# Per-head transposes of a retention and HGRN kernel moved from TensorE to 32x32 turns by VectorE and a permuting DMA

## The reference, cut to what matters

```
s = s * c_dec + einsum('bhjd,bhjv->bhdv', kc * k_dec, vc)                       # retention state
s = exp(b_last)[..., None] * s + einsum('bhjd,bhjv->bhdv', kc * exp(b_last - b), vc)  # HGRN state
o_r = merge(rms_norm(o_rf + flip(o_rb))) * silu(rg)
o_h = merge(rms_norm(o_hf + flip(o_hb), hg_norm_w)) * silu(hg)
out = concatenate([o_r, o_h], axis=-1) @ w_out
y   = rms_norm(x + gate * out, final_norm_w)
```

## Time and profile before

| What | Value |
|---|---|
| Median of 3 runs (lowest to highest) | 1424.56 us (1424.13 to 1424.7) |
| Span of the profiled execution, first to last instruction | 1422.8 us |
| What the runs have around that span | 1.8 us (1424.56 - 1422.8) |
| TensorE busy | 1406.0 us, 99% |
| VectorE busy | 970.9 us, 68% |
| ScalarE busy | 496.9 us, 35% |
| GpSimd busy | 367.9 us, 26% |
| Mean granted TensorE clock | 0.999 of 2.4 GHz |
| DMA of SP's queue | 195.15 MB in 68736 packets, 39.8% of 16 engines |

### The profile page before, as it was taken

The page is one execution under the profiler, slowest core; times in us unless marked ns, Lnnn a source line. Parts: engine busy times, 40 slices in busy tenths (PEclk is TensorE's granted clock), DMA queues, the critical chain, the costliest instruction groups (busy, mean ns, idle before and its releaser), DMA issues.

```text
span 1422.8 us, 24874 instructions
## 1 busy us (share of the span) xinstructions
PE 1406.0 (99%) x10232; PEld 1186.6 (83%) x10232; DVE 970.9 (68%) x1293; ACT 496.9 (35%) x894; POOL 367.9 (26%) x292
## 2 busy tenths in 40 slices
PE   7999999999999999999999999999999999999997
PEld 5788898889888988898889888988898888888886
DVE  5655666666689778877887788866676668632345
ACT  4333343334333433343334233423342334321234
POOL 0000115311532153215321532153115315301220
PEclk9999999999999999999999999999999999999999
DMA  9994222322333334333432343222223347183235
GB/s 387 417 419 148 89 83 82 90 96 67 127 122 123 97 126 133 113 97 126 134 111 97 127 135 110 97 97 90 82 69 96 89 154 254 46 288 111 89 104 206
DMA packets 68870, 196.66 MB, mean 138 GB/s; under 512 B 7824, under 2 KB 16288, under 8 KB 63904
## 3 DMA queue, kind: packets, MB, share of 16 engines
q1 hardware_dynamic: 68736, 195.15, 39.8%
q10 hardware_dynamic: 32, 0.02, 0.0%
HBM read 174.41 MB, written 16.53 MB: 134 GB/s over the span
## 4 chain that ended last, share of the span: by engine, by line
PE 96%; DMA 3%; DVE 1%; SPq 0%; issue 0%; ACT 0%; DVEq 0%; ACTq 0%
PE ps L2044 10%; PE ps L2046 10%; PE ps L2045 10%; PE ps L1867 9%; PE ps L1869 8%; PE ps L1868 8%; PE ps L1843 8%; PE ps L2227 5%; PE ps L2229 5%; PE ps L2228 5%; DMA area<-in_w_mod 3%; PE ps L2061 2%; PE ps L1876 2%; PE ps L1874 2%; PE ps L1875 2%; PE ps L1833 2%
## 5 line engine op out<-in xcount | busy, mean ns | idle before, releaser
L1151 DVE TENSOR_TENSOR w_lo<-area,w_hi 128x1024 fp32r<-128x1024 f32 x143 | 182.9, 1279 | 254.6 <-ACT w_hi L679 254.5
L679 ACT ACTIVATE w_hi<-area 128x1024 fp32r<-128x1024 f32 x143 | 151.6, 1060 | 501.8 <-PE ps L2046 292.5
L2044 PE MATMUL ps<-w_hi,hT_hi 128*128 128x512 f32 x640 | 252.1, 394 | 0.0
L2046 PE MATMUL ps<-w_hi,hT_lo 128*128 128x512 f32 x640 | 249.3, 390 | 0.0
L2045 PE MATMUL ps<-w_lo,hT_hi 128*128 128x512 f32 x640 | 249.3, 389 | 0.0
L1867 PE MATMUL ps<-hT_hi,w_hi 128*128 128x512 f32 x512 | 205.5, 401 | 0.0
L1868 PE MATMUL ps<-hT_lo,w_hi 128*128 128x512 f32 x512 | 199.8, 390 | 0.0
L1869 PE MATMUL ps<-hT_hi,w_lo 128*128 128x512 f32 x512 | 199.7, 390 | 0.0
L2046 PEld LDWEIGHTS ps<-w_hi,hT_lo 128*128 128x128 f32 x640 | 120.1, 188 | 25.4
L1735 POOL TENSOR_TENSOR area<-area 128x320 f32<-128x320 f32 x56 | 53.0, 947 | 339.5 <-PE ps L2061 287.1
L2044 PEld LDWEIGHTS ps<-w_hi,hT_hi 128*128 128x128 f32 x640 | 120.2, 188 | 24.3
(11 more groups left out here) (287 smaller groups left out, 2466.4 us busy)
## 6 DMA issues: line engine op xcount, KB each, us to landing
area<-in_w_in SPq DMA_DIRECT2D x144, 512.0 KB, 4.0
area<-in_w_mod SPq DMA_DIRECT2D x26, 1024.0 KB, 12.4
area<-in_w_out SPq DMA_DIRECT2D x38, 512.0 KB, 3.7
gate_raw<-in_w_gate SPq DMA_DIRECT2D x32, 512.0 KB, 3.7
gate_raw<-in_w_mod SPq DMA_DIRECT2D x6, 1024.0 KB, 12.1
o_hi_scratch<-area SPq DMA_DIRECT2D x14, 320.0 KB, 2.2
o_lo_scratch<-area SPq DMA_DIRECT2D x14, 320.0 KB, 2.9
hT_hi<-o_hi_scratch SPq DMA_DIRECT2D x14, 320.0 KB, 7.4
```

What stands on the lines that cost most here:

```text
L679: act.activation(split_weights(h, n)[0], raw[:, n % 3, :], ACT.Copy).then_inc(wt_hi.sem, 1)
L1151: v.tensor_tensor(lo, raw[:, n % 3, :], hi.bitcast(F32), ALU.subtract).then_inc(wt_lo.sem, 1)
L2044: mm(out, hT_hi[:, k, tile_cols(t)], w_hi[:, n % 2, w], start=k == 0, stop=False)
L2046: i = mm(out, hT_lo[:, k, tile_cols(t)], w_hi[:, n % 2, w], start=False, stop=k == KT - 1)
```

## The change

For heads 0 to 6 the 18 transposes on TensorE go away. Head 7 keeps them. In their place:

- VectorE turns each 32x32 block of the decayed keys in place of its own block (`turn_keys`: 512, 128 and 384 columns into `rope`), at the end of item 17. SP then (`move_keys`, item 4, behind the load of chunk 4) stores `rope` to DRAM (512 KB in rows of 4 KB), waits for it, and reads it back with 4 DMAs that put the blocks in their places in `kltok`, in runs of 32 numbers (128 B), 1024 runs each.
- VectorE turns the 32x32 blocks of the gated outputs (`retention_turn` at item 3, `hgrn_turn` at item 13; 640 columns each) into `o_one`. ScalarE rounds them into `o_two`, VectorE subtracts in place, and SP stores the two parts with 4 DMAs each, one per quarter of the partitions, in runs of 128 B, 640 runs each.
- TensorE does `chunk_updates` behind the retention outputs after chunk 1, and waits there for the moved keys. Waits for the removed pieces go, and some that they carried move to their neighbours.

```
+        k_dram = nc.dram_tensor("key_scratch", (P, 8 * P), F32).ap()
...
+            def store_turned(row, stored):
+                for dram, buf in ((o_hi_dram, o_two), (o_lo_dram, o_one)):
+                    out = dram[bass.ds(row, 1)].rearrange("h (c i) (t q j) -> q i (h t) c j", c=QUARTERS, q=QUARTERS, j=QUAD)
+                    for q in range(QUARTERS):
+                        sp.dma_start(out[q], buf[q * QUAD:(q + 1) * QUAD, :].rearrange("p (t c j) -> p t c j", c=QUARTERS, j=QUAD)
+                                     ).then_inc(stored.sem, 16)
+            def move_keys(h):
+                sp.wait_ge(k_turned.sem, k_turned.at(h))
+                sp.dma_start(k_dram, rope).then_inc(k_moved.sem, 16)
+                sp.wait_ge(k_moved.sem, k_moved.at(h, 16))
+                sp.wait_ge(r_kt.sem, r_kt.at(h))
+                turned = k_dram.rearrange("(q j) (t c i) -> c j t q i", q=QUARTERS, c=QUARTERS, i=QUAD)
+                for c_ in range(QUARTERS):
+                    sp.dma_start(kltok[c_ * QUAD:(c_ + 1) * QUAD].rearrange("p t (q i) -> p t q i", q=QUARTERS), turned[c_]
+                                 ).then_inc(k_moved.sem, 16)
...
                 if n == 4 and prev is not None:
+                    move_keys(prev)
                     store_states(prev, n_ret_f, n_ret_b, rst, r_state, r_state_stored)
...
                 if n == 8 and prev is not None:
-                    sp.wait_ge(r_low.sem, r_low.at(prev))
-                    sp.dma_start(o_hi_dram[bass.ds(prev, 1)].rearrange("h d t -> (h d) t"), o_one).then_inc(r_stored.sem, 16)
-                    sp.dma_start(o_lo_dram[bass.ds(prev, 1)].rearrange("h d t -> (h d) t"), o_two).then_inc(r_stored.sem, 16)
+                    sp.wait_ge(o_split.sem, o_split.at(prev, 1))
+                    store_turned(prev, r_stored)
...
                 if n == 17 and prev is not None:
-                    sp.wait_ge(h_low.sem, h_low.at(prev))
...
+                    sp.wait_ge(o_split.sem, o_split.at(prev))
+                    store_turned(prev + HEADS, h_stored)
...
+            def turned_high(h, k):
+                act.wait_ge(o_turned.sem, o_turned.at(h, k))
+                act.wait_ge(h_silu.sem, h_silu.at(h, 4))
+                act.activation(o_two_r, o_one, ACT.Copy).then_inc(o_rounded.sem, 1)
...
+            def retention_turn(h):
+                dve.wait_ge(r_gated.sem, r_gated.at(h))
+                v.transpose(o_one, sT).then_inc(o_turned.sem, 1)
+            def hgrn_turn(h):
+                dve.wait_ge(h_gated.sem, h_gated.at(h))
+                dve.wait_ge(r_stored.sem, r_stored.at(h))
+                v.transpose(o_one, hsT).then_inc(o_turned.sem, 1)
+            def turned_low(h, k):
+                dve.wait_ge(o_rounded.sem, o_rounded.at(h, k))
+                v.tensor_tensor(o_one_r, o_one, o_two, ALU.subtract).then_inc(o_split.sem, 1)
+            def turn_keys(h):
+                dve.wait_ge(h_kl.sem, h_kl.at(h))
+                v.transpose(rope[:, 0:4 * P], KL[:, 0, 0:4 * P])
+                v.transpose(rope[:, 4 * P:5 * P], KL[:, 1, 0:P])
+                v.transpose(rope[:, 5 * P:8 * P], KL[:, 1, 2 * P:T]).then_inc(k_turned.sem, 1)
...
                     tokens_last(h)
+                    if not isinstance(h, int) or h < HEADS - 1:
+                        turn_keys(h)
...
             def chunk_updates(h):
-                pe.wait_ge(h_kltok.sem, h_kltok.at(h))
+                if h == HEADS - 1:
+                    pe.wait_ge(last_keys.sem, last_keys.at(0))
+                else:
+                    pe.wait_ge(k_moved.sem, k_moved.at(h))
+                    pe.wait_ge(r_S.sem, r_S.at(h))
+                    pe.wait_ge(r_state.sem, r_state.at(h))
...
                     if n == 1:
                         retention_outputs(prev, A, BB)
-                        key_tokens(prev)
-                    if n == 2:
                         chunk_updates(prev)
                     if n == 3:
-                        retention_columns(prev, h)
                         level_scores(prev, h, 0)
                         level_scores(prev, h, 1)
...
-                    if n == 13:
-                        pe.wait_ge(ctx_copied.sem, ctx_copied.at(h))
-                        hgrn_columns(prev, h)
```

More of the change, by code:

```diff
@@ L317, in layer @@
         h_sq, h_rms, h_gated = Signal("h_sq"), Signal("h_rms", 2), Signal("h_gated")
[L318 to L321, removed]
+        last_keys, pe_hu, pe_level = Signal("last_keys", 2), Signal("pe_hu"), Signal("pe_level", PRODUCTS)
+        pe_ho = Signal("pe_ho")
+        h_S0, h_stored, h_state_stored = Signal("h_S0", 32), Signal("h_stored", 2 * QUARTERS * 16), Signal("h_state_stored", 32)
         o_landed = [Signal(f"o_landed{j}", 32 if j % 4 == 3 else 64) for j in range(WCHUNKS)]
@@ L727, in group_columns @@
                     act.wait_ge(pe_group.sem, pe_group.at(h, s + 1))
-                    if due(pe_hkl, h - 1):
-                        act.wait_ge(pe_hkl.sem, pe_hkl.at(h - 1))
+                    if due(k_turned, h - 1):
+                        act.wait_ge(k_turned.sem, k_turned.at(h - 1))
                     act.activation(KL[:, s, P:T], ps[:, GROUP_BANKS[s], :], ACT.Exp, scale=-1.0).then_inc(h_ez.sem, 1)
@@ L812, in keys @@
             def keys(h):
-                act.wait_ge(pe_hkl.sem, pe_hkl.at(h))
+                act.wait_ge(last_keys.sem, last_keys.at(0, 1))
                 act.activation(kltok[:, 0:4, :], tiles(ps[:, C, :]), ACT.Copy)
-                act.activation(kltok[:, 4:8, :], tiles(ps[:, DD, :]), ACT.Copy).then_inc(h_kltok.sem, 1)
+                act.activation(kltok[:, 4:8, :], tiles(ps[:, DD, :]), ACT.Copy).then_inc(last_keys.sem, 1)
             def context_states(h):
@@ L852, in hgrn_high @@
             def hgrn_high(h, out, context):
-                act.wait_ge(pe_ht.sem, pe_ht.at(h))
+                act.wait_ge(pe_columns.sem, pe_columns.at(0))
                 act.activation(out[:, P:T], ps[:, A, :], ACT.Copy)
@@ L887, in items @@
                     if n == 2:
-                        keys(prev)
                         retention_norm(prev, A, BB)
-                    if n == 3:
                         context_states(prev)
                     if n == 4:
-                        retention_high(prev, o_one_r, ctx_columns(h)).then_inc(r_high.sem, 1)
+                        turned_high(prev, 1)
                     if n == 12:
@@ L1440, in items @@
                         hgrn_silu(prev, 3)
+                        retention_turn(prev)
                     if n == 4:
@@ L1460, in items @@
                     if n == 15:
-                        dve.wait_ge(h_high.sem, h_high.at(prev))
-                        hgrn_low(o_one_r, o_two_r, ctx_columns(h)).then_inc(h_low.sem, 1)
+                        turned_low(prev, 2)
                 if prev is None:
@@ L1506, in items @@
                     v.tensor_tensor(strip, strip, ident, ALU.add).then_inc(strip_i.sem, 1)
+                    if prev is not None:
+                        hgrn_turn(prev)
                 if n == 14:
@@ L2094, in retention_columns @@
                     nc.tensor.transpose(ps[:, C, tile_cols(t - 1)], sT[:, tile_cols(t)], ident)
-                nc.tensor.transpose(ctx_columns(following), sT[:, 0:P], ident).then_inc(pe_rt.sem, 1)
+                nc.tensor.transpose(ctx_columns(following), sT[:, 0:P], ident).then_inc(pe_columns.sem, 1)
             def key_tokens(h):
@@ L2129, in level_scores @@
                         pe.wait_ge(r_scaled.sem, r_scaled.at(h))
+                        pe.wait_ge(h_S.sem, h_S.at(h))
+                        pe.wait_ge(h_state.sem, h_state.at(h))
                     q, keys = hq, XE[:, 1, 1, :]
@@ L2134, in level_scores @@
                 if following is not None:
-                    if product == 2:
-                        pe.wait_ge(r_low.sem, r_low.at(h))
                     if product == 4 and 0 <= gate_block(h) < GATE_BLOCKS:
@@ L2165, in hgrn_columns @@
                     nc.tensor.transpose(ps[:, A, tile_cols(t - 1)], hsT[:, tile_cols(t)], ident)
-                nc.tensor.transpose(ctx_columns(following), hsT[:, 0:P], ident).then_inc(pe_ht.sem, 1)
+                nc.tensor.transpose(ctx_columns(following), hsT[:, 0:P], ident).then_inc(pe_columns.sem, 1)
             def stage(n, h, prev):
@@ L2191, in stage @@
                         hgrn_outputs(prev)
-                    if n == 13:
-                        pe.wait_ge(ctx_copied.sem, ctx_copied.at(h))
-                        hgrn_columns(prev, h)
                 if n == 15:
+                    pe.wait_ge(ctx_copied.sem, ctx_copied.at(h))
                     if first_head(h):
-                        pe.wait_ge(ctx_copied.sem, ctx_copied.at(h))
                         pe.wait_ge(h_q.sem, h_q.at(h))
+                    else:
+                        pe.wait_ge(h_gated.sem, h_gated.at(h - 1))
                     pe.wait_ge(roped.sem, roped.at(h))
```

27 lines of the change are left out of this document (8 added, 19 removed).

## The result

The changed kernel takes 1410.12 us (median; 1409.88 to 1410.64), against 1424.6 us for the kernel before: ratio 0.99, 95% interval 0.9886 to 0.9914. That is 14.5 us less; forecast were 13.9 us less and 1410.7 us. The span of the profiled execution fell by 14.6 us, from 1422.8 to 1408.2.

What follows compares the result with a forecast made beforehand. TensorE, 99% busy and never waiting in the heads, was taken to bound the kernel; 126 passes at 0.11 us give 13.9 us, with no new wait at 20 ns a packet: 1424.56 - 13.9 = 1410.7 us, range 1409.5 to 1448.

Steps and rivals of the forecast that it cites:

- What is removed: TensorE, heads 0 to 6: 126 transpose passes at 0.11 us each, 13.9 us less; bounds 11.8 to 15.0.
- a slower matmul behind each group: TensorE: the slow matmul behind each removed group goes too, some 0.08 us x 2 per head; upper bound 15.0 us.
- All that is new is hidden: Likeliest case, all heads: no new wait opens for t up to 25 ns; 1410.7 us, chance 0.50.
- VectorE at the copy's rate: VectorE's key turns of 1024 columns run as fast as a copy: 1.25 us, bounded by 1.2 and 6.9.
- The price of a packet: DMA engine time t per 128-byte packet in output stores and key reading: 20 ns, bounds 14 to 29.
- My line through the packets of 512 and 4096 B: Lower bound of t: 28.6 ns and 162 ns give 0.037 ns a byte, so 14 ns at 128 B.
- my formula: Load 0 lands 3.5 + 0.32 t after the store; loss 0.576 t - 14.6 per transition behind gate heads.
- The slack: At 20 ns: 0.3 us for load 0 behind gate heads, 2.8 us for head 2's keys before the chunk updates.
- That criterion: Head starts: the prediction is wrong if chunk 0's rounding waits for a load.
- The rival that ends slower: SP's queue behind the HGRN store: small packets hold up weight loads from t = 30 ns; 1448 at 36 ns; chance 0.34.
- The rule on small packets: Stores under 512 B cost a read and a write, 58 ns a packet: 1471 us; chance 0.10 of the slower 0.34.
- The keys late through the turn: VectorE's key turn at the reciprocal's rate, 5.6 us later: 20 us lost, 1430; chance 0.03, inside the slower 0.34.

Runs made afterwards that it cites:

- experiment 3: Changed kernel with the transpositions of heads 0 to 6 left out: no turns, no key moving, outputs stored unturned with two DMAs of whole rows; 1409.77 us.
- experiment 5: Changed kernel with the HGRN output store of heads 0 to 6 done twice, the second to scratch in the same 128-byte runs; 1441.84 us.
- experiment 6: Changed kernel with a second HGRN output store to scratch, 8 DMAs more per head in runs of 512 B; 1425.88 us.
- 7: Changed kernel with doubled HGRN output stores, for heads 0 to 5 issued behind loads 0 and 1 of the next head; 1415.1 us.
- experiment 8: Changed kernel with head 7's keys also turned by VectorE and moved by SP behind the first output weight loads; 1411.06 us.
- experiment 9: Changed kernel with a second 512 KB store of the turned keys ahead of the real one, each waited for; 1421.33 us.

## Why the prediction was right, and where it was right for the wrong reason

- **What is removed.** Right: TensorE waits for nothing in the heads, so a pass is worth its distance. Forecast 13.9 us (bounds 11.8 to 15.0), measured 14.5. Between the starts of heads 2 and 7 the change takes 10.21 us (707.69 - 697.48) for 90 passes, 0.113 each. Some 0.4 us of the 14.6 by which the span fell lies ahead of the heads, where the change does nothing: the first product of the HGRN queries (L1843, now L1886) starts at 116.97 instead of 117.38. I had put a slower matmul behind each group into the upper bound. The output columns, which stand in two groups of five per head, gave most per pass (0.122), which fits, but was not tried.
- **All that is new is hidden.** Right, and shown by experiment 3: 0.35 us by the medians, 0.1 us a head by the traces. VectorE at the copy's rate was right too (1.28 us for 1.25). The Trainium skill's page "VectorE: DVE Perf Modes" (The three transpose paths) gives 311 ns for a 128x128 bf16 tile; here the 128 fp32 columns took 0.27 us, and all eight 1.28 instead of 2.5. The same section warns that a plain DMA copy with strides for a transpose is 19 times slower than the transposing one when the innermost destination stride is large. Here the innermost runs are 32 numbers in a row, so that warning isn't put to the test: the reading back of 512 KB landed some 6 us after its issue, a plain load of that size takes 3.5.
- **The price of a packet was too high, and a term was missing; the two nearly cancel, which is luck.** I priced t = 20 ns (bounds 14 to 29) as work of the DMA engines. It is 12.9 ns in the stores' stretch, just below my bounds. My line through the packets of 512 and 4096 B, which gave 14 ns, was nearly right, and I should have taken it. With 12.9 ns and no issue time I would have put the rounding of chunk 0 at 7.6 us after the store (3.5 + 0.32 x 12.9); it was at 10.37. What takes the rest is SP's issuing: 6.1 to 6.6 us for 8 DMAs. I had the 8 DMAs in the text and gave their issue no term, although a plain issue of 0.33 us stands in the earlier trace rows. With 20 ns my formula has 9.9, only 0.5 us short of what was measured. The time came out right because more slack was left than the 0.3 us of my sum (next but one).
- **In the reading back the packets' price does count.** SP's queue on the engines in 340:343:

```profile
q1 hardware_dynamic: 3393, 0.44, 95.7%
```

Here the engines are busy nearly all the time, at 13.5 ns a packet. So one half of my argument (the keys) was bound by what I had named, and the other half (the outputs) by SP.
- **The slack.** At gate heads I forecast 0.3 us at 20 ns, counted to the rounding of chunk 0. The rounding came 0.8 us late, and I had written that I would be wrong if it waited for a load. That criterion was wrong: TensorE needs not the rounding but the copy behind it, and 2.6 us were left there (experiment 5). For the keys I forecast 2.8 us at 20 ns, and 1.3 were left in head 2. There the key store took 6.5 us instead of 3.6 (331.45 to 337.99), the reading back some 6 instead of 7.3. At the true price of a packet my formula would have given 4.6 us (7.9 - 0.256 x 12.9), so the term that was too small is mostly the key store.
- **The rival that ends slower** (the output stores hold up the weight loads) is a real mechanism at the place that I named, and was not reached. Experiment 5 reached it by doubling one of the two stores of each head; 6 and 7 showed that it hangs on SP's queue. Fitted afterwards, my formula gives its waits: with a t of 40 ns for that store and 21 for the keys it has 4 x 3.6 + 2 x 1.8 + 4.3 = 22.3 us, and the new waits are 22.1. That is luck. Neither t is the price of a packet, and the slack of 2.5 us that it uses up last is the keys' (7.9 - 0.256 x 21), which was 1.3; what TensorE waited for was the copy, with 2.6. What the formula lacked besides is the granted clock behind the longer waits, some 10 us.
- **The rule on small packets.** By the Trainium skill, "DMA: Bandwidth & Descriptors" (Specifications), transfers below 512 B make an SDMA engine read, modify and write; I worked out 58 ns a packet and 1471 us. The rows show 12.9 ns a packet for stores of 128 B, less than the 28.6 ns of a packet of 512 B: if it happens, it costs nothing that can be seen here.
- **The keys late through the turn**: not in heads 0 to 6. In head 7 (experiment 8), where the change leaves the keys on TensorE, the turn does cost time, but through what stands behind it on VectorE, and not through late keys.

What stays open: how the time of one issue divides between the number of runs and the shape of the pattern (below), and in part why the key store takes so long. Over the seven heads it landed 5.0 to 6.5 us after its issue, with load 4 issued just ahead of it. The second key store of experiment 9, issued once the first had landed, took 2.6 us in six heads and 3.6 in one. So about half is the queue ahead; why head 2 has 1.2 us more than the others is open.

## What to carry to other kernels

Where TensorE never waits, each pass taken from it is worth its distance between starts; the question is only which path gets late, and the way to know its slack is to read when the data lands against its first use, or to double one suspect and read the first wait. Count DMA instructions, not bytes alone: eight DMAs in place of two hold the issuing queue for some six microseconds, and what stands behind them is late by that, so new ones belong behind the loads that others wait for, or where the queue is idle. Measure a slack to where the bounding engine itself needs the data, not to the first engine that is seen to wait. And look at every head: here the keys had 1.3 us in the head that I had worked out, and 0.8 in the tightest. Before times of two traces are compared, take off by how much the whole stretch has moved.

## What the runs showed of the hardware that I had not expected

- **The time to issue one DMA depends on its number of runs, but weakly.** SP in the changed kernel (duration of one issue in ns, lowest, median and highest):

```profile
L499 SPq DMA_DIRECT2D o_hi_scratch<-area x56: 583/642/1701, 235.1 to 1146.5; - x56
...
L510 SPq DMA_DIRECT2D area<-key_scratch x28: 575/683/1315, 197.6 to 1036.5; - x28
```

A store of 640 runs of 128 B takes 0.64 us, a read of 1024 runs 0.68, the key store of 128 rows 0.43 (331.45), and the stores of 160 runs in experiment 6 about 0.5 (1.91 for four).
- **A 128-byte packet costs a DMA engine about 13 ns**, in stores (12.9 in 449.5:456.5) as in reads (13.5 in 340:343), where a 512-byte one is at 28.6 by the earlier trace rows and a 4096-byte one at 162 by the earlier trace rows. So a quarter of the bytes costs not quite half the time.
- **The clock after a short wait.** Behind a wait of 3.45 us a pair of passes took 0.53 us instead of 0.29 for some 3 us; the granted clock of the 8 us behind it was 0.79 (experiment 5). Behind waits of about 2 us it went both ways: 0.79 behind the 2.2 us at 754.57 in experiment 6, 1.00 behind the 2.2 us at 770.79 in experiment 9.
